# Gated feed-forward with a three-tap convolution: taps applied with the tokens on the partitions instead of the features

## What is computed

```python
def depthwise_conv_centred(h, w, b):          # three taps over the tokens
    hp = jnp.pad(h, ((0, 0), (1, 1), (0, 0)))
    out = b
    for t in range(3):
        out = out + hp[:, t:t + S] * w[t]
    return out

def conv_gated_ffn(h, w_up, conv_w, conv_b, w_down):   # w_up: 2048 x 11264, w_down: 5632 x 2048
    a = depthwise_conv_centred(h @ w_up, conv_w, conv_b)
    g, u = jnp.split(a, 2, axis=-1)
    return (jax.nn.silu(g) * u) @ w_down
```

## Time and profile before

| | us |
|---|---|
| median of 3 runs (3382.36 to 3386.32) | 3382.86 |
| profiled execution, time | 3384.2 |
| profiled execution, span from first to last instruction | 3382.4 |
| TensorE matmuls busy | 3352.6 (99%) |
| VectorE busy | 2054.3 (61%) |
| ScalarE busy | 1618.3 (48%) |
| GpSimd busy | 116.1 (3%) |
| HBM traffic over the span | 177 GB/s |

### The profile page before, as it was taken

One profiled execution on the slowest core, in us unless ns is written; L12 is line 12 of the kernel. 1 busy time (PEld: TensorE's weight loads), 2 busy tenths in 40 slices (PEclk: granted clock), 3 DMA queues, 4 the chain that ended last, 5 costly groups with the idle time before them and its releaser, 6 DMA issues.

```text
span 3382.4 us, 44153 instructions
## 1 busy us (share of the span) xinstructions
PE 3352.6 (99%) x17976; PEld 2885.7 (85%) x17976; DVE 2054.3 (61%) x1893; ACT 1618.3 (48%) x1632; POOL 116.1 (3%) x82
## 2 busy tenths in 40 slices
PE   8999999999999999999999999999999999999999
PEld 8998888888888998888888888989989888888887
DVE  5755565566656655656565656567777555555555
ACT  4554544444444464544444445437644544444443
POOL 0110000000000120000000000010020000000000
PEclk9999999999999999999999999999999999999999
DMA  7345555555554435555555554433354455555554
GB/s 264 126 149 186 183 191 186 186 186 188 188 192 176 146 127 185 187 187 188 192 188 187 189 186 162 180 124 138 137 199 150 162 187 187 191 192 186 186 193 167
DMA packets 85990, 600.52 MB, mean 178 GB/s; under 512 B 9392, under 2 KB 11488, under 8 KB 14192
## 3 DMA queue, kind: packets, MB, share of 16 engines
q1 hardware_dynamic: 84128, 591.43, 49.1%
q0 software_dynamic: 1744, 7.34, 0.6%
HBM read 596.64 MB, written 2.10 MB: 177 GB/s over the span
## 4 chain that ended last, share of the span: by engine, by line
PE 95%; DVE 3%; ACT 1%; DMA 0%; issue 0%; SPq 0%; DVEq 0%
PE ps L493 24%; PE ps L495 24%; PE ps L494 24%; PE ps L461 6%; PE ps L462 6%; PE ps L463 6%; PE ps L502 2%; DVE w_lo L1651 1%; PE ps L585 0%; PE ps L574 0%; PE ps L656 0%; ACT scores_h L1151 0%; PE ps L544 0%; DVE scores_h L1743 0%; ACT scores_h L1162 0%
## 5 line engine op out<-in xcount | busy, mean ns | idle before, releaser
L1130 ACT ACTIVATE w_hi<-w_raw 128x2048 fp32r<-128x2048 f32 x558 | 1067.2, 1914 | 1136.1 <-DMA w_raw<-in_weights 1136.1
L1651 DVE TENSOR_TENSOR w_lo<-w_raw,w_hi 128x2048 fp32r<-128x2048 f32 x558 | 1279.3, 2297 | 492.8 <-ACT w_hi L1130 492.1
L493 PE MATMUL ps<-w_hi,actb_hi 128*128 128x512 f32 x1920 | 749.4, 390 | 0.0
L495 PE MATMUL ps<-w_lo,actb_hi 128*128 128x512 f32 x1920 | 747.1, 389 | 0.0
L494 PE MATMUL ps<-w_hi,actb_lo 128*128 128x512 f32 x1920 | 747.1, 389 | 0.0
L461 PE MATMUL ps<-act_hi,w_hi 128*128 128x256 f32 x1728 | 502.4, 291 | 16.3 <-DVE act_lo L1668 9.1
L462 PE MATMUL ps<-act_lo,w_hi 128*128 128x256 f32 x1728 | 491.9, 285 | 0.0
L463 PE MATMUL ps<-act_hi,w_lo 128*128 128x256 f32 x1728 | 491.6, 284 | 0.0
L493 PE MATMUL ps<-w_hi,h_hi 128*128 128x512 f32 x1216 | 476.4, 392 | 0.0
L495 PE MATMUL ps<-w_lo,h_hi 128*128 128x512 f32 x1216 | 473.4, 389 | 0.0
L494 PE MATMUL ps<-w_hi,h_lo 128*128 128x512 f32 x1216 | 473.3, 389 | 0.0
(11 more groups left out here) (327 smaller groups left out, 2725.2 us busy)
## 6 DMA issues: line engine op xcount, KB each, us to landing
w_raw<-in_weights SPq DMA_DIRECT2D x558, 1024.0 KB, 4.8
w_raw<-in_weights SPq DMA_DIRECT2D x4, 512.0 KB, 8.3
x_features<-in_xT SPq DMA_DIRECT2D x4, 512.0 KB, 8.6
x_stream<-in_x POOLq DMA_DIRECT2D x1, 2048.0 KB, 11.7
mem_sb<-in_mem POOLq DMA_DIRECT2D x4, 512.0 KB, 5.0
out_x<-x_stream SPq DMA_DIRECT2D x4, 512.0 KB, 2.8
w_s_sb<-in_w_s POOLq DMA_DIRECT2D x2, 512.0 KB, 8.6
consts_sb<-in_consts POOLq DMA_DIRECT2D x1, 686.5 KB, 8.5
```

The lines of the kernel that those rows point to most:

```text
L493: mm(o, a_hi, hi, start=first and c == 0, stop=False)
L495: end = mm(o, a_hi, lo, start=False, stop=last and c == 3)
L1130: A(w_hi[:, s], w_raw[:, s], ACT.Identity).then_inc(hi_done, 1)
L1651: tt(w_lo[:, s], w_raw[:, s], hi_of(w_hi[:, s]), ALU.subtract).then_inc(w_ready, 1)
```

## The change

After it, the convolution is done where `copy` leaves the values, with tokens on the partitions.

* The neighbours come by transfers inside the core's memory. For each half GpSimd's queue issues four: partitions 0 to 126 of `gr` or `ur` to partitions 1 to 127 of `prev` (127 rows of 4 KB), one row of 2 KB across the border of the two token groups, and the same two the other way to `next_`. The rows outside the sequence are set to zero once per layer.
* A tap is now one value per column. Each half's three tap rows and its bias row (8 KB in HBM) are loaded to all 128 partitions (`rows_of`, 1 MB written), by GpSimd's queue, when the previous block's same half has been convolved.
* VectorE does all six operations of a half, each `tensor_tensor` over 128 x 1024: three products (`tap_products`) and three sums (`tap_sums`). ScalarE's `base` is gone.
* Silu and the product with the up half are made in place, and only the product is transposed: one group of eight transposes per block (`hidden_turned`), in the next block after piece 1 (block 0's after piece 3 of block 1; block 10's in the middle of its own piece 11). `hidden_hi` and `hidden_lo` read it from the banks.
* In the last block VectorE does `tap_products` of the up half ahead of the addition of down piece 8, and `hidden_lo` after the addition of piece 11 and the last split.

```diff
 @block.gpsimd
+                def rows_of(b, half):
+                    n = C0 + 2 * b + half
+                    src = conv_rows[n:n + 1, :].to_broadcast([P, 4 * 512])
+                    pool.dma_start(rows[half][:].rearrange("p a c -> p (a c)"), src).then_inc(rows_in[half], 16)
+                def shifted(b, half):
+                    pool.wait_ge(up_copied, C0 + 2 * b + half + 1)
+                    src, before, after = (gr, ur)[half], prev[half], next_[half]
+                    pool.dma_start(before[1:P], src[0:P - 1]).then_inc(shift_in[half], 16)
+                    pool.dma_start(before[0:1, 1], src[P - 1:P, 0]).then_inc(shift_in[half], 16)
+                    pool.dma_start(after[0:P - 1], src[1:P]).then_inc(shift_in[half], 16)
+                    pool.dma_start(after[P - 1:P, 0], src[0:1, 1]).then_inc(shift_in[half], 16)
+                pool.wait_ge(acc_done, l * LAYER_PIECES + P_FF)
+                for half in range(2):
+                    for edge in (prev[half], next_[half]):
+                        G.memset(edge[:], 0.0).then_inc(edges_zero, 1)
...
+                for b in range(BLOCKS1):
+                    for half in range(2):
+                        shifted(b, half)
+                        if b + 1 < BLOCKS1:
+                            pool.wait_ge(conv_done, C0 + 2 * b + half + 1)
+                            rows_of(b + 1, half)
 @block.tensor
-                def turned_up(b, half):
-                    pe.wait_ge(up_copied, U0 + 2 * b + half + 1)
-                    turned(4 + 2 * half, (gr, ur)[half], 0).then_inc(up_turned, 1)
+                def hidden_turned(b):
+                    pe.wait_ge(h_ready, H0 + b + 1)
+                    turned(4, ur, 0).then_inc(up_turned, 1)
...
-                            if half == 0 and q == 0 and first:
-                                turned_up(b - 1, 1)
-                            elif half == 1 and q == 0:
-                                pe.wait_ge(conv_done, U0 + 2 * b - 1)
-                                turned_up(b, 0)
+                            if half == 0 and q == (3 if first else 1):
+                                hidden_turned(b - 1)
                     pe.wait_ge(h_split, H0 + b)
                     for j in range(DOWN):
+                        if j < 2:
+                            pe.wait_ge(up_copied, U0 + 2 * b + j + 1)
                         pe.wait_ge(added, D1 + 4 * (b - 1) + j - 1)
-                        tokens(p + UP1 + j, j, (h_hi[:, 1 - par], h_lo[:, 1 - par]), 0, 2 * (j % 2))
-                        if j == 0:
-                            pe.wait_ge(conv_done, U0 + 2 * b)
-                            turned_up(b, 1)
+                        tokens(p + UP1 + j, j, (h_hi[:, 1 - par], h_lo[:, 1 - par]), 0, 2 * (j % 2),
+                               between=(lambda: hidden_turned(b)) if last and j == 3 else None)
 @block.scalar
-                def base(b, half):
-                    act.wait_ge(up_turned, U0 + 2 * b + half + 1)
...
+                def step1(b, par, first=False, last=False):
+                    p = F0 + UP1 + (b - 1) * (UP1 + DOWN)
                     for k in range(UP1):
                         tick(p + k, k % 4)
+                        if k == (5 if first else 2):
                             hidden_hi(b - 1, 1 - par)
+                        if k == 3:
                             copy(b, 0, p + 4)
+                        elif k == 7:
                             silu(b)
                             copy(b, 1, p + 8)
                     for k in range(DOWN):
                         tick(p + UP1 + k, k)
+                    if last:
+                        hidden_hi(b, par)
 @block.vector
+                row = lambda half, t: rows[half][:, t:t + 1, :].to_broadcast([P, TB, 512])
+                def tap_products(b, half):
+                    dve.wait_ge(rows_in[half], 16 * (H0 + b + 1))
+                    dve.wait_ge(shift_in[half], 64 * (H0 + b + 1))
+                    dst = (gr, ur)[half]
+                    tt(prev[half][:], prev[half][:], row(half, 0), ALU.mult)
+                    tt(next_[half][:], next_[half][:], row(half, 2), ALU.mult)
+                    step(tt(dst[:], dst[:], row(half, 1), ALU.mult))
+                def tap_sums(b, half, terms):
+                    dst = (gr, ur)[half]
+                    for t in terms:
+                        term = (prev[half][:], next_[half][:], row(half, 3))[t]
+                        last = tt(dst[:], dst[:], term, ALU.add)
...
                     for k in range(UP1):
                         tick(p + k, k % 4)
...
+                        if k == (2 if first else 0):
                             gated_hidden(b - 1)
+                        elif k == (5 if first else 2):
                             hidden_lo(b - 1, 1 - par)
+                        if k == 5:
+                            tap_products(b, 0)
+                        elif k == 6:
+                            tap_sums(b, 0, range(3))
                     for k in range(DOWN):
+                        if last and k == 0:
+                            tick(p + UP1, 0)
+                            tap_products(b, 1)
+                        add_plain(p + UP1 + k, k)
+                        if not last or k:
+                            tick(p + UP1 + k, k)
                         if last and k == 1:
+                            tap_sums(b, 1, range(3))
                             gated_hidden(b)
                         elif not last and k == 1:
+                            tap_products(b, 1)
                         elif not last and k == 2:
+                            tap_sums(b, 1, [0])
                         elif not last and k == 3:
+                            tap_sums(b, 1, [1, 2])
+                    if last:
+                        hidden_lo(b, par)
```

More of the change, by code:

```diff
@@ L95, with build @@
 S_END = S_FF2 + 4 * BLOCKS2
-UPS2 = 2 * LAYERS * BLOCKS1
-def build(nc, x, xT, weights, wdt, params1, params2, consts, consts1, w_s, b_s, mem, positions, out):
+UPS2 = LAYERS * BLOCKS1
+UPC2 = 2 * LAYERS * BLOCKS1
+def build(nc, x, xT, weights, wdt, params1, params2, consts, consts1, conv_rows, w_s, b_s, mem, positions, out):
     ctx = ExitStack()
@@ L155, in build @@
         ur = at("up_tokens", [TB, 512], F32, AA + 4 * KB)
[L156 to L159, removed]
+        prev = [at(n, [TB, 512], F32, AA + (8 + 4 * i) * KB) for i, n in enumerate(("gate_prev", "up_prev"))]
+        next_ = [at(n, [TB, 512], F32, AA + (16 + 4 * i) * KB) for i, n in enumerate(("gate_next", "up_next"))]
+        hm = at("hidden", [4, T], F32, AA + 8 * KB)
         x_fm = at("x_features", [KC, T], F32, HA)
@@ L169, in build @@
         sqk1 = fixed("sqk1", [10, T])
+        rows = [at(n, [4, 512], F32, o) for n, o in (("gate_rows", AA + 24 * KB), ("up_rows", SK))]
         pt1 = at("pt1", [TB, 4, T], F32, SK)
@@ L482, in factor_row, with tokens @@
                 mm(ps[:, 7, 0:T], ones, tmp[:], start=True, stop=True).then_inc(row_ready, 1)
-            def tokens(p, s, acts, c0, bank, first=True, last=True):
+            def tokens(p, s, acts, c0, bank, first=True, last=True, between=None):
                 pe.wait_ge(w_ready, p + 1)
                 for b in range(TB):
+                    if b and between is not None:
+                        between()
                     o = ps[:, bank + b, :]
@@ L1348, in up @@
                             copy(b, 0, p + 4)
-                        elif k == 5:
-                            base(b, 0)
-                        elif k == 6:
+                        elif k == 7:
                             silu(b)
-                        elif k == 7:
                             copy(b, 1, p + 8)
-                def step1(b, par, first=False, last=False):
-                    p = F0 + UP1 + (b - 1) * (UP1 + DOWN)
-                    up(p, b, par, first)
                     for k in range(DOWN):
-                        if last and k == 1:
-                            base(b, 1)
@@ L1362, in step1 @@
                         tick(p + UP1 + k, k)
-                        if last and k == 1:
-                            hidden_hi(b, par)
-                        elif k == 1:
-                            base(b, 1)
+                    if last:
+                        hidden_hi(b, par)
                 tick(F0, 0)
@@ L1922, in _ @@
                 F0, U0, H0, D1 = P0 + P_FF, 2 * l * BLOCKS1, l * BLOCKS1, D0 + 8
-                col = lambda b, c, half, t: prm1[:, bass.ds(M0 + C_CONV + b * 32 + (2 * c + half) * 4 + t, 1)]
-                def taps(b, half, t):
-                    dst, bank = (ga, ua)[half], 4 + 2 * half
-                    src = lambda c: ps[:, bank + c // 2, c % 2 * T + t:c % 2 * T + t + T - 1]
-                    for c in range(4):
-                        if t == 0 and c % 2 == 0:
-                            dve.wait_ge(conv_base, 2 * U0 + 4 * b + 2 * half + c // 2 + 1)
-                        out = dst[:, c, 1 - t:T - t]
```

(18 more changed lines are left out.)

78 lines of the change are left out of this document (31 added, 47 removed).

## The result

The changed kernel takes 3442.33 us (median of 4 runs, 3438.56 to 3453.57) against 3383.09 us (4 runs, 3382.36 to 3386.32) for the kernel before: ratio 1.0178, 95% interval 1.0159 to 1.0197. It is slower by 59 us, where 3380.4 was forecast, and outside the forecast range.

What follows compares the result with a forecast made beforehand. TensorE, busy 99% of the span, was taken to bound the kernel. Transposes saved 19.1 us and last-block waits cost 16.6 over both layers, a net -2.5 us: forecast 3380.4 us, range 3370 to 3402.

Steps and rivals of the forecast that it cites:

- TensorE's work: Two groups of transposes per block removed, one added: 22 groups less over two layers, 19.1 us saved.
- The shift latency S: Time from `up_copied` to the landing of a half's four transfers: taken as 7.5 us, bounds 5.0 and 11.7.
- A loop block: The 16 loop blocks: nothing waits, 0 us, with 0.6 us a block as the upper bound.
- the 0.15 us to spare: Loop block, piece 12: VectorE's split ends at 10.5 us, TensorE's weight load asks at about 10.65.
- the first rival: TensorE waits at each of 16 to 20 loop blocks if piece 12's slack is missing: 11 us, 3391; chance 0.14.
- The head of a layer: Zero fills, first row loads and block 0's up half, convolved in block 1, are covered: taken as 0 us.
- A load slowed by 3 us stays inside that: Weight loads: ready 9 us after issue, asked for after 16.3, so a 3 us slowdown causes no wait.
- (a): Last block of a layer: up-half products delay down piece 8's addition, so TensorE waits 3.2 us at down piece 10.
- (b): Last block of a layer: `hidden_lo` stands behind piece 11's addition and a split; down pieces wait 5.0 us, whatever S.
- The late landing: Neighbours land late at the gate half's `tap_products`; with S = 12.5 some 3425 us; chance 0.06.
- Its extreme: Transfers of 127 partitions run on one engine: 21 us a half over 22 blocks, about +900, 4270 us; chance 0.08.
- The last block's waits are smaller: Rival: (a) and (b) do not show, 3363.7 us, or 3371 with S at 5 and half of (b); chance 0.12.

Runs made afterwards that it cites:

- e1: Changed kernel with GpSimd issuing the next block's row loads behind both halves' neighbour transfers, same bytes; 3399.91 us, ratio 1.0048 to the kernel before.
- x1: e1 plus block 0's `hidden_turned` one piece later and last-block additions, splits and `hidden_lo` moved earlier on VectorE; 3376.03 us, ratio 0.9982 to the kernel before.

## Why the prediction was wrong

- **TensorE's work: right.** 22 x 0.87 = 19.1 us went, and a loop block takes 66.2 us wherever nothing waits (e1, x1). VectorE's six operations cost 1.22 us each, and its share of the span is 64% (66% forecast; 66% in x1).
- **The shift latency S: right for one half only.** 7.5 us was taken, between 5.0 and 11.7. In the changed kernel's loop the gate half's last packet ends 7.4 to 8.7 us after the copy, and VectorE starts 8.4 to 9.8 us after it. The up half's last packet ends after 13 to 18 us, beyond the upper bound. The step that failed is "Up half: ... covered as long as S is under 12.9": the limit was right (in e1, where nothing waits, VectorE starts the products up to 12.9 us after the copy), but the same S was put into it. "The DMA engines' share rises from 53% to about 71%" (measured: 74%) was an average over a block of something that comes in bursts. The rows' load had its bytes counted and not its moment, although the order of GpSimd's queue in the diff gives it: the gate's sums end just ahead of the up half's copy.
- **A loop block, 0 us (0.6 a block as the upper bound): wrong,** 30.3 us in 17 waits on `w_lo`, for the reason above and not because the 0.15 us to spare was missing. With the load behind, the tight stretch from place 10 on holds (e1, x1): the first rival fell.
- **The head of a layer, 0 us: wrong,** 14.5 us in 2 waits. Block 0's up neighbours reached VectorE 15 to 17 us after the copy in the changed kernel, where 7.6 was assumed; with the load behind them it is 9.5 to 10.2 us, and e1 still waits 8.1 us there. A second step failed with it: "A load slowed by 3 us stays inside that". In e1 a weight load beside the neighbours was slowed by 7 us (11.9 against 4.8), and the split that it held up stood ahead of the sums. `hidden_turned` one piece later takes most of the wait away (x1: 2.4 us).
- **The last block, (a) 3.2 us: 4.1 us,** a term mis-sized by S: the last packet ends 7.8 us after the copy, about as taken, but VectorE starts only at 8.9, where 7.6 was counted. **(b) 5.0 us: 4.7 us** of idle time, and 5.04 us from matmul to matmul: right, though it costs more than itself.
- **The clock: missing.** "Nothing behind recovers it" was right and too kind: ten of the waits come with 3.4 to 10.2 us at half speed, some 21 us in all. No row of before had such a wait in these stages, so the price could not be read there. Outside them there was a sign: a wait of 2.3 us and some small matmuls in the trace of before are followed by 6.6 us of work at 0.50, from 2230.6 us on. As a bound from above the clock should have stood in the sum.
- **The rivals.** The late landing, 3425 at a chance of 0.06, came nearest, but its place was given as the gate half with both halves alike. Its extreme, one engine for 127 partitions, is refuted: 508 KB lands in 5.7 us, where one engine would take 23. From 731 to 733 us of the changed kernel's span only packets of GpSimd's queue are in flight, the gate half's neighbours, and the DMA view of that window has the 16 engines fully busy with them: `q0 software_dynamic: 171, 0.52, 101.0%` (packets, MB, share of 16 engines' time). The Trainium skill's "DMA: Bandwidth & Descriptors" names this exception in its section on why a DMA increments its semaphore by 16, and the trace agrees with the exception. "The last block's waits are smaller" fell with (a) and (b).
- **The sum with the missing terms:** -19.1 + (14.5 + 30.3 + 8.2 + 9.3) + 21 = +64, measured +69.4 in that execution. Of the last 5 us some 4 are the length of the waits themselves, by an estimate: a wait shifts TensorE by its idle time and the 0.39 us of the matmul before it, less the 0.23 us after which the next one would have started, so 0.16 us more than the list has, in 23 waits. The rest is not assigned.

## What to carry to other kernels

Count an added transfer by its moment and not by its share of the bandwidth: write down which transfer leaves just ahead of it and which weight loads fall beside it, and ask who waits for the last of them; a load that nobody needs soon should leave when nothing urgent is about to. Where TensorE is saturated, price a new wait of some us at its length plus half of the work in the half-speed stretch behind it (2.6 us for a wait of 5 us here). And when an in-order engine waits for a transfer, look at the additions and splits queued behind the wait, since moving those, and block 0's transposes by one piece, won 23.9 us here (e1 to x1), more than the 19.1 us of work that the change removed.

## What the runs showed of the hardware

- The granted clock falls from 2.4 to 1.2 GHz behind a single wait of TensorE in an otherwise full stream. In the changed kernel's two feed-forwards nine waits took 3.2 to 9.1 us (from matmul start to matmul start), and each came with 3.4 to 10.2 us at half speed; of the eight of 1.3 to 2.9 us only one did (2.7 us). The length of the stretch is not fixed by that of the wait: 5.04 us gave 3.4 us at 1054.4 and 6.8 us at 2129.6 in one execution.
- A transfer of 127 partitions issued by GpSimd uses all 16 engines (their share is 101% from 731 to 733 us, with its packets alone; 508 KB land in 5.7 us).
- A weight load of 1 MB that goes out beside a half's neighbours and a row load lands after up to 12.4 us, where it takes 4.8 in the kernel before.
- Four transfers of one half, 1.04 MB, are seen by VectorE 8.4 to 9.8 us after the copy where no row load leaves ahead of them (the gate halves of the changed kernel's loop; the least outside it is 7.3), of which some 2 us is GpSimd's issuing (0.50 to 0.53 us each) and about 1 us lies behind the last packet.
- Orders of GpSimd's queue with the same bytes lie 144 us apart: 3399.9 us (loads behind both halves), 3442.3 (one ahead), 3544.1 (both ahead).
